# Modulation sums moved from TensorE to GpSimd, gate projection cut into eight steps, expert start rearranged

## What is computed

```python
# block 1
mod = silu(c) @ w_ada + b_ada                  # 1024 x 3072
h = rms_norm(x, norm_g) * (1 + scale) + shift
proj = h @ w_in                                # r, k, v, gate g, lora; q, k, v, gate of attention
# RWKV-7 recurrence over r, decay, k, v (8 heads of 64), group norm, bonus, times silu(g_r)
# chunk-band attention (8 heads), times silu(g_a)
x = x + gate * (y @ w_out)
# block 2
mod2 = silu(c2) @ ada_w + ada_b                # 1024 x 6144
# hybrid mixer (state-space model, forgetting attention, convolution), then
h = rms_norm(x) * (1 + sc_f) + sh_f
x = x + g_f * hierarchical_moe(h)              # 32 experts of width 512, 2 for each row
return rms_norm(x) * final_norm_g
```

## Time and profile before

| | us |
|---|---|
| median of 3 runs | 1393.48 |
| the profiled execution | 1391.97 |
| its span | 1389.9 |
| PE busy | 1292.5 (93%) |
| DVE, ACT, POOL busy | 559.7, 351.2, 160.5 |
| granted TensorE clock, mean | 0.982 |

### The profile page before, as it was taken

The page is one execution under the profiler, slowest core; times in us unless marked ns, Lnnn a source line. Parts: engine busy times, 40 slices in busy tenths (PEclk is TensorE's granted clock), DMA queues, the critical chain, the costliest instruction groups (busy, mean ns, idle before and its releaser), DMA issues.

```text
span 1389.9 us, 21101 instructions
## 1 busy us (share of the span) xinstructions
PE 1292.5 (93%) x7560; PEld 640.0 (46%) x7561; DVE 559.7 (40%) x1034; ACT 351.2 (25%) x759; POOL 160.5 (12%) x278
## 2 busy tenths in 40 slices
PE   5999999999999998999999998999999987897777
PEld 1445656568954444554445545433333333332222
DVE  1366363655214333349786635312212212121115
ACT  1223231422135442221467510101111101110102
POOL 4011010101120000000000001411121111111110
PEclk9999999999999999999999999999999999999999
DMA  9250704323163110014112384789999999999995
GB/s 365 84 212 11 279 26 167 138 79 149 35 187 147 46 46 1 0 49 167 52 57 76 122 348 182 276 350 396 411 412 419 399 406 421 403 402 416 409 391 209
DMA packets 40420, 303.93 MB, mean 219 GB/s; under 512 B 7964, under 2 KB 8116, under 8 KB 22800
## 3 DMA queue, kind: packets, MB, share of 16 engines
q1 hardware_dynamic: 31808, 285.12, 52.3%
q0 software_dynamic: 8528, 17.67, 4.1%
HBM read 299.49 MB, written 13.75 MB: 225 GB/s over the span
## 4 chain that ended last, share of the span: by engine, by line
PE 74%; DMA 14%; DVE 6%; issue 2%; ACT 2%; POOL 1%; DVEq 0%; SPq 0%; ACTq 0%; POOLq 0%
PE bank L858 21%; PE bank L2874 12%; DMA arena<-in_w_down 11%; PE bank L790 8%; PE bank L2892 7%; PE bank L904 4%; PE bank L969 2%; PE bank L847 2%; PE bank L2862 2%; DMA arena<-in_ada_w 1%; PE bank L1186 1%; PE bank L1130 1%; PE bank L1107 1%; PE bank L893 1%; PE bank L2883 1%
## 5 line engine op out<-in xcount | busy, mean ns | idle before, releaser
L858 PE MATMUL bank<-hT,arena 128*128 128x512 f32 x720 | 320.0, 599 | 0.0
L2874 PE MATMUL bank<-arena,hT 128*64 128x512 f32 x1024 | 231.9, 603 | 18.0 <-DMA arena<-in_w_gu 17.6
L858 PEld LDWEIGHTS bank<-hT,arena 128*128 128x128 f32 x720 | 135.0, 191 | 162.6 <-issue 159.2
L2874 PEld LDWEIGHTS bank<-arena,hT 128*64 128x64 f32 x1024 | 72.9, 138 | 156.3 <-issue 138.1
L2892 PE MATMUL bank<-arena,yT 128*64 128x512 f32 x512 | 123.8, 628 | 15.7 <-DMA arena<-in_w_down 13.9
L790 PE MATMUL bank<-arena,yT 128*128 128x512 f32 x256 | 114.5, 601 | 2.4 <-DVE yT L1685 2.3
L3062 DVE TENSOR_SCALAR hT<-hT 128x256 f32<-128x256 f32 x32 | 9.4, 295 | 248.4 <-ACT hT L3000 248.4
L3000 ACT ACTIVATE hT<-bank 128x256 f32<-128x256 f32 x32 | 12.3, 384 | 264.0 <-PE bank L2874 264.0
L790 PEld LDWEIGHTS bank<-arena,yT 128*128 128x128 f32 x256 | 48.1, 192 | 60.0 <-issue 56.2
L2892 PEld LDWEIGHTS bank<-arena,yT 128*64 128x64 f32 x512 | 36.1, 143 | 78.7 <-issue 61.2
L904 PEld LDWEIGHTS bank<-arena 64*64 64x64 f32 x1856 | 59.3, 135 | 23.8 <-issue 14.4
(11 more groups left out here) (489 smaller groups left out, 1609.1 us busy)
## 6 DMA issues: line engine op xcount, KB each, us to landing
arena<-in_w_gu SPq DMA_DIRECT2D x63, 2048.0 KB, 26.8
arena<-in_w_down SPq DMA_DIRECT2D x32, 2048.0 KB, 30.5
arena<-in_w_in SPq DMA_DIRECT2D x53, 512.0 KB, 4.6
arena<-in_ada_w SPq DMA_DIRECT2D x24, 1024.0 KB, 5.1
arena<-in_w_ada SPq DMA_DIRECT2D x8, 1024.0 KB, 9.1
arena<-in_w_out SPq DMA_DIRECT2D x8, 1024.0 KB, 9.0
arena<-in_w_ada SPq DMA_DIRECT2D x8, 512.0 KB, 4.7
arena<-expert_rows SPq DMA_DIRECT2D x4, 1024.0 KB, 8.4
```

Source lines behind the costliest of these rows:

```text
L858: last = T.matmul(bank[0:rows, :], w[:, k, 0:rows], hT[:, k, :], start=k == 0, stop=k == KD - 1)
L2874: last = T.matmul(banks[1 + ub][MT * h:MT * h + MT, :], tile.xT[:, k, :], wgu[u][:, k // 4, k % 4, :, 256 * h:256 * h + 256], start=k == 0 ...
```

## The change

1. The modulation groups 2 to 4 leave PE's steps. POOL multiplies each 128x2048 chunk by its column of silu(c2) in place (`mod_part`, `tensor_scalar`) and adds it to a running sum in SBUF (`tensor_tensor`): 8 multiplications and 7 additions a group, in pairs 0, 1 and 2. Parts 0, 1 and 2 stand ahead of the waits for masks 3, 4 and 5, parts 3 to 7 behind `mod_io`. PE adds up the 128 partitions with a product by ones early in the next pair (`mod_rows`), and DVE adds the bias there (`mod_made`).
2. The gate projection of a pair is no longer made a pair ahead as one block. Its eight matmuls go one by one at levels 4 and 5, at level 6, and through the chunks of the pair itself (`gate_steps`); in pair 3 two at each of levels 1 to 4. Level 4 of pairs 0 to 2 loses the projection. Ahead of pair 0, projection g goes, and the order of the norms changes.
3. The first gathers of the experts and the first two of the extra tile read their indices from `slots` directly (`gather_known`), with no copy and no wait for it.
4. The first slot's gate and up weights are loaded again by quarters after the first product (`first_next_gate_up`), each released when two or four of the eight steps are done.
5. Two small DVE instructions of the router go behind the hot positions.

```diff
@@ POOL, a part of the sums, and the pair's loop
+            def mod_part(g, k):
+                n = KD * g + k
+                slot, turn = ada_slot(n)
+                c = cact[:, KD + k:KD + k + 1]
+                eng.wait_ge(ada_sem[slot], 16 * (turn + 1))
+                if k:
+                    done(G.tensor_scalar(ada_slots[slot], ada_slots[slot], c, None, MUL))
+                    done(G.tensor_tensor(mod_sum, mod_sum, ada_slots[slot], ADD))
+                else:
+                    if g > 2:
+                        eng.wait_ge(filled, fill_at[("mod", g - 1)] + 1)
+                    done(G.tensor_scalar(mod_sum, ada_slots[slot], c, None, MUL))
+                eng.sem_inc(s_ada_used, 1)
...
                 for l in range(1, LEVELS - 1):
                     if l > 2:
+                        if p + 1 < PAIRS:
+                            mod_part(2 + p, l - 3)
                         eng.wait_ge(filled, fill_at[("W", p, l - 2)] + 1)
...
                 mod_io(1 + p)
+                if p + 1 < PAIRS:
+                    for k in range(LEVELS - 4, KD):
+                        mod_part(2 + p, k)
@@ PE
+                def gate_steps(count):
+                    name = ("proj", p, 3)
+                    if not p and not gate_k[0]:
+                        eng.wait_ge(s_mod, 2)
+                    w = chunk_ready(name)
+                    for _ in range(count):
+                        k = gate_k[0]
+                        gate_k[0] += 1
+                        bank = fill(name) if k == KD - 1 else begin(name)
+                        last = T.matmul(bank[:, :], w[:, k, :], hT[:, k, :], start=k == 0, stop=k == KD - 1)
+                        if k == KD - 1:
+                            full(last)
+                def mod_rows(g):
+                    eng.wait_ge(s_ada_used, KD * (g + 1))
+                    bank = fill(("mod", g))
+                    for j in range(4):
+                        last = T.matmul(bank[32 * j:32 * j + 32, :], ones[:, 0:32], mod_sum[:, 512 * j:512 * j + 512],
+                                        start=True, stop=True)
+                    full(last)
...
                 if p:
                     mean(p - 1)
-                if not q:
-                    eng.wait_ge(s_mod, 5)
-                ada_step()
+                    mod_rows(1 + p)
                 va_rows(1)
...
-                    if l <= 4 and q:
+                    if l <= 3 and q:
                         pe_proj(("proj", q, PROJ_ORDER[l - 1]))
-                    elif q and l == LEVELS - 2:
-                        ada_step()
+                    elif q:
+                        gate_steps(1)
                     else:
+                        if l <= 4:
+                            gate_steps(2)
                         va_rows(2 if l <= 4 else 1)
@@ PE ahead of pair 0
             lora(0)
+            key_norm(0)
             pe_proj(("proj", 0, 2))
-            key_norm(0)
             eng.wait_ge(s_first_in, 1)
-            for k in range(3):
-                pe_ada(1, k)
-            pe_proj(("proj", 0, 3))
-            for k in range(3, KD):
+            for k in range(KD):
                 pe_ada(1, k)
@@ DVE in the pair
                 gram_masked(p, 2, LbT, 1)
                 if p:
+                    gate_clamp(p - 1)
                     center(p - 1)
+                    mod_made(1 + p)
                 level_add(p, 1)
...
                 level_add(p, 4)
-                if q:
-                    proj_shift(q, 3)
+                if not q:
+                    proj_shift(p, 3)
...
-                eng.wait_ge(s_yg, p + 1)
-                dve_clamp(("gate", p), t_g)
                 if q:
-                    dve_ada(2 + p)
+                    proj_shift(p, 3)
+                else:
+                    gate_clamp(p)
@@ DVE ahead of pair 0
             decay_clamp(0)
+            key_norm_in(0)
+            decays(0)
+            bonus_in(0)
             proj_shift(0, 2)
-            decays(0)
-            key_norm_in(0)
-            bonus_in(0)
-            proj_shift(0, 3)
             operands(0)
@@ SP, when the chunks of the sums are issued
-        ada_after = {("proj", 0, 3): KD + 1, ("proj", 1, 3): KD, ("proj", 2, 3): KD, ("proj", 3, 3): KD - 1}
+        ada_after = {("proj", 0, 2): KD}
+        for p in range(PAIRS - 1):
+            then = [("proj", p + 2, j) for j in PROJ_ORDER[:3]] if p + 2 < PAIRS else [("va", 0), ("proj", PAIRS - 1, 3), ("va", 1)]
+            for name, count in zip([("proj", p, 3)] + then, (3, 1, 2, 2)):
+                ada_after[name] = ada_after.get(name, 0) + count
@@ SP, first release
+            def first_next_gate_up(u, e):
+                p, n = slot_before(e)
+                eng.wait_ge(more_.gate_up, n + 1)
+                stand_alone(eng)
+                for half, (steps_done, at) in enumerate(((first.half_done, 1), (first.gate_up, 2))):
+                    eng.wait_ge(s_slots, SLOTS + 1 + half)
+                    load_quarter(u, e, half, 0, w_gu[u][half])
+                    eng.wait_ge(steps_done, p + at)
+                    stand_alone(eng)
+                    load_quarter(u, e, half, 1, w_gu[u][half])
@@ POOL, first gathers
+            def gather_known(tile, e):
+                eng.indirect_dma_start(tile.xg, None, xn_dram, bass.IndirectOffsetOnAxis(ap=slots[:, e:e + 1], axis=0),
+                                       bounds_check=SEQ - 1, oob_is_err=False).then_inc(tile.gathered, 16)
...
             for u in range(U):
                 eng.wait_ge(tiles[u].xf, 1)
-                gather(tiles[u], u, FIRST[u], s_picked[0], u)
+                gather_known(tiles[u], FIRST[u])
@@ DVE, router
-            done(V.reciprocal(wts[:, 0, :], r_w1))
-            done(V.tensor_tensor(wts[:, 1, :], wts[:, 0, :], r_d, MUL))
...
             V.tensor_copy(ov_first[:, KEPT_AT:KEPT_AT + NE - 3], r_kept)
+            done(V.reciprocal(wts[:, 0, :], r_w1))
+            done(V.tensor_tensor(wts[:, 1, :], wts[:, 0, :], r_d, MUL))
```

More of the change, by code:

```diff
@@ L161, in plan, with plan_on @@
             fills.append((name, by))
+        def plan_on(name, by, bank):
+            held[name] = bank
+            plan(name, by)
+            free_banks[0].remove(bank)
         def plan_proj(p, j):
@@ L198, in build_program @@
                 plan(("W", p, l), "act")
-                if l <= 4 and q:
+                if l <= 3 and q:
                     plan_proj(q, PROJ_ORDER[l - 1])
+                if l == 4 and not q:
+                    plan_on(("proj", p, 3), "act", ADA_BANK)
+                    free_banks[0].append(ADA_BANK)
                 if l in (2, 4) and not q:
@@ L504, in add_chunk2, with add_proj, add_va @@
             add_chunk(A["w_in_2"][W_IN2_BLOCKS.index((name, i))], (name, i))
-        for p in range(PAIRS):
-            for j in PROJ_ORDER:
+        def add_proj(p, js):
+            for j in js:
                 add_chunk(A["w_in"][(j * D_RWKV + p * P) // P], ("proj", p, j))
+        def add_va(n):
+            add_chunk(A["w_in"][(AT0 + 2 * 512 + n * P) // P], ("va", n))
         AT0 = 4 * D_RWKV + 128
-        for n in range(4):
-            add_chunk(A["w_in"][(AT0 + 2 * 512 + n * P) // P], ("va", n))
+        add_proj(0, PROJ_ORDER[:3])
+        for p in range(1, PAIRS):
+            add_proj(p, PROJ_ORDER[:3])
+            add_proj(p - 1, PROJ_ORDER[3:])
+        add_va(0)
+        add_proj(PAIRS - 1, PROJ_ORDER[3:])
+        for n in range(1, 4):
+            add_va(n)
         for p in range(PAIRS):
@@ L1271, in out_norm, with gate_exp @@
                 eng.sem_inc(s_rn, 1)
+            def gate_exp(p):
+                if p + 1 < PAIRS:
+                    eng.wait_ge(s_ops, 3 * (p + 1) + 1)
+                eng.wait_ge(s_shift, ITEM[p, 3] + 1)
+                act.done(S.activation(t_g, gsh[:, p % 2, :], ACT.Exp, scale=-1.0))
+                eng.sem_inc(s_yg, 1)
             proj_raw(0, 1)
@@ L1297, in act_block1 @@
                 if p:
-                    act_sigmoid(("gate", p - 1), (t_g, None))
+                    gate_exp(p - 1)
                 for l in range(1, LEVELS):
@@ L1303, in act_block1 @@
                     if l == 1 and p:
+                        act_sigmoid(("gate", p - 1), (t_g, None))
                         out_square(p - 1)
@@ L1306, in act_block1 @@
                         key_square(q)
-                    if l <= 4 and q:
+                    if l <= 3 and q:
                         proj_raw(q, l - 1)
+                    if l == 4 and not q:
+                        proj_raw(p, 3)
                     if l in (2, 4) and not q:
@@ L1330, in act_block1 @@
                 if q:
-                    eng.wait_ge(s_ops, 3 * q + 1)
-                act.done(S.activation(t_g, gsh[:, p % 2, :], ACT.Exp, scale=-1.0))
-                eng.sem_inc(s_yg, 1)
+                    proj_raw(p, 3)
+                else:
+                    gate_exp(p)
                 bank = take(S, ("Y", p))
@@ L1399, in act_block1 @@
```

(17 more changed lines are left out.)

77 lines of the change are left out of this document (44 added, 33 removed).

## The result

The changed kernel takes 1502.38 us (median, 1491.20 to 1502.67) against 1393.92 for the kernel before in the same session (1389.54 to 1395.79): a ratio of 1.0763, 95% interval 1.0734 to 1.0791. Slower was right, and the range of 1425 to 1530 holds it; the forecast of 1479 is 23 us short.

What follows compares the result with a forecast made beforehand. PE, busy for 93% of the span, was taken as the bound. Terms 81.0 + 5.1 - 4.9 - 2.0 + 8.1 - 0.4 = +86.9 on 1391.97 gave 1479 us, range 1425 to 1530.

Steps and rivals of the forecast that it cites:

- parts 0 to 2: Early modulation parts on POOL: no price beside DVE's PSUM reads; part 2 makes W of level 3 2.3 us late.
- ahead of pair 0: Before the first pair: the gate projection goes and pair 0's transposes start earlier, -4.9 us (bounds -7.1 and 0).
- pair 3: Last pair, where PE waits for nobody: eight gate steps 7.0 us and `mod_rows` 1.05, +8.1 (bounds +4 and +8.1).
- The multiplication's price: POOL's 128x2048 multiplication: taken as 2.0 us, near the copy, between bounds of 1.9 and 4.55.
- The main term: Parts 3 to 7 at levels 3 and 4: ten DVE instructions each wait for one of POOL's; +81.0 us in three pairs.
- PE after a pause: Slower PE products behind the long stall, 1.7 us once a pair: +5.1 us (bounds 0 and 10).
- Rival 3: `operands` in levels 3 and 4: long POOL instructions do not keep DVE waiting, so faster, 1382 us; chance 0.12.
- rival 4: In the pairs: a little hold-up of DVE, 3 us a pair, cancels the gain, 1392 us; chance 0.05.
- Rival 1: POOL's multiplications in the pairs are as dear as additions, 4.55 us: +38 us, 1517 us; chance 0.12.
- rival 2: In the pairs: a POOL multiplication holds nothing up, only additions hold DVE: +42 us, 1434 us; chance 0.16.
- Rival 5: The change does not do what it says, for the gathers and quarters: 2 us at most; no chance given.
- The lead lost in the experts: Expert loads: quarters let SP's queue resume some 2.1 us earlier, but the lead is lost: 0 (bounds -2.1 and 0).

Runs made afterwards that it cites:

- no_sums: The changed kernel with POOL's multiplications and additions of the modulation parts left out, every wait, DMA and PE step kept: 1390.0 us.
- adds_only: The changed kernel without POOL's multiplications of parts 1 to 7, so chunks are summed unscaled: 1456.2 us.
- writes_only: The changed kernel with each POOL multiplication and addition replaced by memsets of about its length, which write SBUF and read nothing: 1405.1 us.
- experts_only: The kernel before with only the expert part of the change (direct gathers, router instructions moved, loads by quarters): 1391.0 us, ratio 0.9984.

## Why the prediction was right, and where its sizes were not

The mechanism and the sign stand: GpSimd's long instructions hold back VectorE's, the lateness reaches PE at levels 3 to 5 of pairs 0 to 2, and taking the arithmetic away gives it all back. The table sets the sum's terms against the trace (span to span: +110.7 where +86.9 was forecast).

| step | forecast | measured |
|---|---|---|
| parts 0 to 2, three pairs: W of level 3 late | 6.9 | 23.9 |
| parts 3 to 7, three pairs: from there to W of level 5 | 76.5 | 72.6 |
| three pairs, from W of level 5 on: gate steps and pauses | +2.7 | +2.4 |
| chunk waits that go | -2.0 | in the rows above |
| three pairs in all | 84.1 | 98.9 |
| ahead of pair 0 | -4.9 | -5.8 |
| pair 3 | +8.1 | +14.5 |
| from attention to the end | -0.4 | +3.0 |

- **The multiplication's price** is the first mis-sized term: 2.0 taken, 5.6 measured. The nearer row was the one that I set aside, 713 ns for 192 columns in the earlier trace rows: it is the same operation, and less the 0.18 it scales to (0.713 - 0.18) x 2048 / 192 + 0.18 = 5.9 us. I took the copy's, because it also streams one input. Rows of the same operation go before rows of the same shape of operands.
- **The main term came out right in part by luck.** I had ten held instructions of DVE between 206.5 and 245.1 (38.6 us); there are seven long ones, from 238.46 to 275.8 (37.3 us). Dearer multiplications and fewer turns nearly cancelled.
- **Parts 0 to 2** are where most of the shortfall lies. I priced them at 2.3 us a pair, for part 2 alone: part 0 I put at nothing because VectorE reads PSUM beside it, and part 1 does not appear in the sum at all. In pair 1, at full price they are three multiplications and two additions, and hold L1505 (4.08 us), L1559 (4.88), L1618 (4.08) and L1505 again (4.49). W of level 3 begins 40.6 us into the pair (232.25) instead of 32.9. In three pairs that is 17 us more than forecast, out of 23.8 from span to span; pair 3 and the rest of the kernel add 9.8, and the other terms take 3.0 off.
- **PE after a pause** was put at 5.1, once a pair. PE's busy time in pairs 0 to 2 is 233.0 us, and 217.6 in the kernel without sums, with the same matmuls, so 15.4 more. There are three pauses of 7.6 to 16.5 us in pair 1, not one. The mean granted clock of these stages is 0.82 to 0.83, where it was 1.00: around the first pause of pair 1 it is 1.00 up to 225 us, 0.50 from 228 to 236 us, so for some 4 us behind the pause too, and 1.00 again from 240 us. That is the lower of PE's two levels, 1.2 GHz in place of 2.4. But little of it reaches the span, as the slow products behind the first two pauses are done well ahead of the next wait for DVE. What counts is the stretch from W of level 5 to the end of the pair: 27.3, 29.2 and 26.9 us, where kernels with the same steps need 25.15, 25.4 and 25.15 at the least (no_sums in pairs 0 and 1, adds_only in pair 2). These 7.7 us lie within my bounds of 0 and 10; that the gate steps bring 5.3 and not 2.4 makes up for the difference.
- **Pair 3**: PE is busy there for 79.2 us in place of 69.4, so 9.8 more where the sum had 8.1, and the first gate step needs bank 7, which `mod_made(4)` on DVE has still to empty; PE waits 4.8 us for it. I had looked at what `mod_rows` waits for and not at what waits for the bank that it fills.
- **The rivals.** Rival 3 (1382) and rival 4 (1392, with 3 us a pair) are refuted by the held instructions. Rival 3 could not be had without them either: had I priced GpSimd's work right, 77 us and the masks' 8 in a pair of 77, I would have seen that it does not fit, and writes_only, with shorter work and hardly a hold-up, takes 1405. Its base was off as well: the kernel without sums stands at a first product of 881.3, not at 867. Rival 1 (1517) had the price nearly right and the hold wrong; rival 2 (1434) has the hold wrong: a multiplication does hold, a two-input instruction for 3.7 us. Rival 5 was part of the forecast, and experts_only does not contradict it.
- **The lead lost in the experts.** The quarters let SP's queue resume 2.0 us after the first product's start in place of 3.9, and the expert stretch is 514.2 against 513.1, no shorter, as foretold:

```profile
988.39 5.54 SPq L2783 DMA_DIRECT2D arena<-in_w_gu  x4
```

Left open: where the 3.0 us from attention to the end come from. Of these 1.9 lie ahead of the first product, and that stretch differs from 481.6 to 485.0 us among the kernels here, single executions all, so they may be no more than the spread.

## What to carry to other kernels

Work moved to a "free" GpSimd has two prices: its own length against the stage it must fit into (here 86 us in a pair of 77), and each of its instructions that reads SBUF, for which a VectorE instruction with two SBUF inputs waits in turn (and its one-input `tensor_scalar` on SBUF for multiplications, additions and memsets alike). The idle share on a page shows neither; write down both sums before moving anything, and take the price from a row of the same operation. Where VectorE does the same in one pass (2.35 us here against 10.2), it is better to put it there, in pauses that the timeline shows (dve_sums_gate3, 1389.6 us in place of 1502.4, with the gate projection of pair 3 put back).

## What the runs showed of the hardware

- On GpSimd a multiplication by a column's scalar over 128x2048 takes 5.63 us, more than an addition of two tensors (4.58), and the same product written with a broadcast tensor takes 3.73. VectorE needs 2.35 us for the product and the addition together.
- Beside the one-input form VectorE's two-input instructions get through about 1.9 us before the end of its record, beside the two-input forms only at the end. VectorE's one-input `tensor_scalar` on SBUF waits to the end of both (4.08 and 4.49 us in place of 0.43).
- GpSimd's memsets of 2048 columns hold VectorE's two-input instructions up not at all (0.69 us beside six of them), but its one-input `tensor_scalar` does wait for them (1.07 us in place of 0.43 on average).
- Even a VectorE instruction of 3 columns waits for a whole GpSimd instruction (4.47 us instead of 0.15).
